# One stream from the output projection through the FFN norm to the first three up units

## The reference

```python
for l in range(DEPTH):                      # DEPTH = 2
    h = pre_mod(x, mix_pre_g[l], sh1, sc1)  # rms_norm(x, g) * (1 + scale) + shift
    y, yc = mixer(h, hc, ...)               # ends in  concat @ w_out  (1024 x 1024)
    x = post_add(x, y, mix_post_g[l], g1)   # x + gate * rms_norm(y, g)
    f = conv_ffn(pre_mod(x, ffn_pre_g[l], sh2, sc2), ffn_w_up[l], ...)
    x = post_add(x, f, ffn_post_g[l], g2)
    # layer 0 does the same for the context tokens xc; layer 1 only reads them
def conv_ffn(h, w_up, conv_w, conv_b, w_down):
    u = h @ w_up                            # 1024 x 5376
    u = three-tap convolution of u along the tokens, plus conv_b
    a, b = split(u, 2)
    return (gelu(a) * b) @ w_down
```

## Time and profile before

| | us |
|---|---|
| median of 3 runs | 1652.82 (1651.49 to 1652.85) |
| the profiled execution, its own time | 1657.06 |
| its span | 1655.3 |
| TensorE busy | 1518.8 |
| VectorE, ScalarE, GpSimd busy | 968.6, 728.8, 596.9 |

### The profile page before, as it was taken

One profiled execution on the slowest core, in us unless ns is written; L12 is line 12 of the kernel. 1 busy time (PEld: TensorE's weight loads), 2 busy tenths in 40 slices (PEclk: granted clock), 3 DMA queues, 4 the chain that ended last, 5 costly groups with the idle time before them and its releaser, 6 DMA issues.

```text
span 1655.3 us, 22238 instructions
## 1 busy us (share of the span) xinstructions
PE 1518.8 (92%) x7560; PEld 1216.7 (74%) x7560; DVE 968.6 (59%) x1465; ACT 728.8 (44%) x1240; POOL 596.9 (36%) x529
## 2 busy tenths in 40 slices
PE   6889798889999999998999698889988899999998
PEld 1777466667888888886888577677776688887886
DVE  2448577557678666833334566688775544444455
ACT  3432466535323333323353445377774544443453
POOL 1342244233222222322333531364442444443454
PEclk9999799999999999999999899899999899999999
DMA  8120750104355344411122112010001233332232
GB/s 329 47 84 13 248 188 25 51 1 132 123 178 153 115 126 140 127 39 39 63 66 63 53 52 80 25 50 1 1 1 51 77 102 89 101 98 67 83 96 101
DMA packets 129135, 143.85 MB, mean 87 GB/s; under 512 B 7160, under 2 KB 95484, under 8 KB 129064
## 3 DMA queue, kind: packets, MB, share of 16 engines
q1 hardware_dynamic: 129064, 142.91, 27.6%
HBM read 140.79 MB, written 2.10 MB: 86 GB/s over the span
## 4 chain that ended last, share of the span: by engine, by line
PE 79%; DVE 8%; ACT 5%; POOL 3%; issue 2%; DMA 2%; SPq 0%; POOLq 0%; DVEq 0%; ACTq 0%
PE ps L462 22%; PE ps L463 22%; PE ps L464 22%; PE ps L1400 3%; PE ps L1386 2%; PE ps L1411 1%; ACT pT_hi L1451 1%; DVE hT_lo L781 1%; DVE hT_hi L779 1%; ACT prob L1440 1%; DMA start_w<-in_ada_w_dram 1%; PE ps L1413 1%; PE ps L666 1%; DVE o_tmp L1516 1%; DMA ada_w<-in_ada_w_dram 1%
## 5 line engine op out<-in xcount | busy, mean ns | idle before, releaser
L454 POOL TENSOR_TENSOR w_lo<-raw,w_hi 128x1024 fp32r<-128x1024 f32 (+1 forms) x184 | 348.0, 1893 | 644.9 <-ACT w_hi L447 644.9
L462 PE MATMUL ps<-hT_hi,w_hi 128*128 128x512 f32 (+1 forms) x1072 | 383.6, 358 | 7.3 <-DVE hT_lo L781 6.4
L463 PE MATMUL ps<-hT_lo,w_hi 128*128 128x512 f32 (+1 forms) x1072 | 381.2, 356 | 0.0
L464 PE MATMUL ps<-hT_hi,w_lo 128*128 128x512 f32 (+1 forms) x1072 | 378.8, 353 | 0.0
L447 ACT ACTIVATE w_hi<-raw 128x1024 fp32r<-128x1024 f32 (+1 forms) x200 | 172.9, 866 | 190.4 <-PE ps L464 166.6
L462 PEld LDWEIGHTS ps<-hT_hi,w_hi 128*128 128x128 f32 x1072 | 202.8, 189 | 46.6 <-DVE hT_lo L781 10.0
L464 PEld LDWEIGHTS ps<-hT_hi,w_lo 128*128 128x128 f32 x1072 | 202.0, 188 | 29.7
L463 PEld LDWEIGHTS ps<-hT_lo,w_hi 128*128 128x128 f32 x1072 | 202.7, 189 | 27.8
L2053 DVE TENSOR_TENSOR g_lo<-act_g,g_hi 128x768 fp32r<-128x768 f32 (+1 forms) x84 | 106.7, 1277 | 164.2 <-ACT g_hi L2003 162.9
L462 PE MATMUL ps<-w_hi,g_hi 128*128 128x512 f32 x420 | 166.0, 395 | 3.5 <-DVE g_lo L2053 3.0
L464 PE MATMUL ps<-w_hi,g_lo 128*128 128x512 f32 x420 | 164.0, 390 | 0.0
(11 more groups left out here) (234 smaller groups left out, 2497.0 us busy)
## 6 DMA issues: line engine op xcount, KB each, us to landing
raw<-in_ffn_w_up_dram SPq DMA_DIRECT2D x84, 512.0 KB, 3.9
ada_w_up<-in_ada_w_dram SPq DMA_DIRECT2D x48, 512.0 KB, 4.1
raw<-in_ffn_w_down_dram SPq DMA_DIRECT2D x84, 256.0 KB, 2.6
ada_w<-in_ada_w_dram SPq DMA_DIRECT2D x32, 512.0 KB, 5.0
start_w<-in_ada_w_dram SPq DMA_DIRECT2D x8, 1024.0 KB, 11.4
raw<-in_c_w_qkv_dram SPq DMA_DIRECT2D x12, 512.0 KB, 3.6
raw<-in_ab_w_in_dram SPq DMA_DIRECT2D x8, 512.0 KB, 4.1
raw<-in_ab_w_out_dram SPq DMA_DIRECT2D x8, 512.0 KB, 3.8
```

Of the source, the lines that this page charges most:

```text
L454: by.tensor_tensor(w_lo[:, slot, 0:width], raw[:, n % RAW, 0:width], w_hi[:, slot, 0:width].bitcast(F32), ALU.subtract).then_inc(lo_split, 1)
L462: nc.tensor.matmul(outp, s_hi, m_hi, start=first, stop=False, skip_group_check=True)
L463: nc.tensor.matmul(outp, s_hi, m_lo, start=False, stop=False, skip_group_check=True)
L464: return nc.tensor.matmul(outp, s_lo, m_hi, start=False, stop=last, skip_group_check=True)
```

## The change

In both layers the two barriers between the output projection and the up units are gone, with the functions that stood between them (`norm_*` for the FFN, `up_prefetch`, `up_first`).

- The last two second halves, (1,4) and (1,5) in layer 0, (1,2) and (1,3) in layer 1, are made together, chunk by chunk, so that the slots of units 4, 5 and 6 come free at chunks 1, 3 and 5; ScalarE splits up units 0 to 2 into them.
- The norm is cut into 12 steps in layer 0 (8 of the four latent tiles, one chunk each; 4 of the two context tiles, two chunks each) and 8 in layer 1 (4 of tiles 0 and 1, 4 of tiles 2 and 3, two chunks each). Each is 4 transposes into one of banks 6, 7, 5. The first three stand within the last batch of the projection.
- TensorE makes the chunks of the first tiles for up units 0, 1 and 2 together, then the rest of unit 0, unit 1, unit 2.
- Every engine's order of the tiles' tails, steps and splits is written out.
- SyncE waits for the gate's last use in place of the barrier.
- In attention VectorE does O ahead of the T before it.

```diff
+def norm_steps(l):
+    if l == 0:
+        return ([((0, 1, 2, 3), 0, k, 1) for k in range(KC)] + [((4, 5), 1, k, 2) for k in range(0, KC, 2)])
+    return [(tiles, 0, k, 2) for tiles in ((0, 1), (2, 3)) for k in range(0, KC, 2)]
...
+def outputs_first(steps):
+    out = list(steps)
+    for n in range(len(out) - 2):
+        if out[n][0] == "T" and out[n + 2][0] == "O":
+            out[n:n + 3] = [out[n + 2], out[n], out[n + 1]]
+    return out
 def attn_vector(dve, l, before):
     groups, steps, first = attn_setup(l)
+    steps = outputs_first(steps)
...
     if l == 1:
-        return [[(1, 0), (1, 1)], [(0, 3)], [(1, 2)], [(1, 3)]]
-    return [[(0, t)] for t in range(OUT_DONE[l], nt)] + [[(1, t)] for t in range(nt)]
+        return [[(1, 0), (1, 1)], [(0, 3)], [(1, 2), (1, 3)]]
+    return [[(0, 4)], [(0, 5)], [(1, 0)], [(1, 1)], [(1, 2)], [(1, 3)], [(1, 4), (1, 5)]]
...
-GATE_BEHIND = (1, 0)
-OUT_BANKS = (0, 1, 2, 3, 4, 5)
+OUT_BANKS = ((1, 3, 0, 2, 4, 5, 1, 3), (0, 2, 4, 1, 3))
+TURN_BANKS = (6, 7, 5)
+TURN_BEHIND = ({5: 0, 6: 1, 7: 2}, {3: 0, 4: 1, 5: 2})
+MID_TILES = (((0, 1, 2, 3), (4, 5)), ((0, 1), (2, 3)))
...
+def mid_turn(pe, l, j):
+    tiles, _, k0, nk = norm_steps(l)[j]
+    tag, w = f"ffn{l}", len(tiles) * P
+    pe.wait_ge(s("norm_xn"), norm_base(tag, "xn") + tiles[-1] + 1)
+    if j >= 3:
+        pe.wait_ge(s("norm_split"), norm_base(tag, "split") + 2 * (j - 2))
+    for i in range(nk):
+        k = k0 + i
+        for n, t in enumerate(tiles):
+            mm = nc.tensor.transpose(bank(TURN_BANKS[j % 3])[:, i * w + n * P:i * w + (n + 1) * P],
+                                     xn[:, t, k * P:(k + 1) * P], ident[:, :])
+    mm.then_inc(s("norm_turned"), 1)
...
+    for n, batch in enumerate(batches):
+        last = n == len(batches) - 1
+        for half, t in batch:
+            if l == 0 and half == 1 and t >= LAT_T:
+                pe.wait_ge(s(f"{tag}_y0"), t + 1)
...
+            if last and k in (1, 3, 5):
+                mm.then_inc(s(f"out{l}_w_used"), 1)
+            if l == 1 and n == 0 and k == 1:
+                gates()
+            if last and k in TURN_BEHIND[l]:
+                if TURN_BEHIND[l][k] == 0:
+                    pe.wait_ge(s(f"{tag}_gate"), 4 if nt == ALL_T else 2)
+                mid_turn(pe, l, TURN_BEHIND[l][k])
+        if l == 0 and n == 1:
+            gates()
...
+def up_first_tensor(pe, l):
+    phase = f"up{l}"
+    steps = norm_steps(l)
+    first = len([g for g in steps if g[0] == MID_TILES[l][0]])
+    def product(u, j, i):
+        tiles, _, k0, _ = steps[j]
+        k, c0, w = k0 + i, tiles[0] * P, len(tiles) * P
+        kk = slice(k * P, (k + 1) * P)
+        return mm3(bank(2 * u, 1024)[:, c0:c0 + w], w_hi[:, u, kk], w_lo[:, u, kk],
+                   hT_hi[:, k, c0:c0 + w], hT_lo[:, k, c0:c0 + w], k == 0 and c0 % BANK == 0, k == KC - 1)
+    for j in range(first):
+        mid_wait_split(pe, l, j)
+        for i in range(steps[j][3]):
+            for u in range(3):
+                if j == 0 and i == 0:
+                    wait_split(pe, phase, u)
+                product(u, j, i)
+        if l == 0 or j + 3 < first:
+            mid_turn(pe, l, j + 3)
+    if l == 1:
+        for j in range(first, first + 3):
+            mid_turn(pe, l, j)
+    for u in range(3):
+        for j in range(first, len(steps)):
+            if u == 0:
+                mid_wait_split(pe, l, j)
+            for i in range(steps[j][3]):
+                mm = product(u, j, i)
+            if u == 0 and j == first:
+                mid_turn(pe, l, first + 3)
+        mm.then_inc(used[phase], 1)
+def mid_shift(act, l, j):
+    tiles, v, k0, nk = norm_steps(l)[j]
+    w = len(tiles) * P
+    act.wait_ge(s("norm_turned"), norm_base(f"ffn{l}", "turned") + j + 1)
+    for i in range(nk):
+        k = k0 + i
+        h = bank(TURN_BANKS[j % 3])[:, i * w:(i + 1) * w]
+        op = nc.scalar.activation(h, h, ACT.Identity, bias=add_col[:, 1, v, k:k + 1],
+                                  scale=mul_col[:, 1, v, k:k + 1])
+    op.then_inc(s("norm_h32"), 1)
...
+def mid_split(dve, l, j):
+    dve.wait_ge(s("norm_h32"), norm_base(tag, "h32") + j + 1)
+    nc.vector.tensor_copy(hT_hi[:, kk, c0:c0 + w], h).then_inc(s("norm_split"), 1)
+    dve.wait_ge(s("norm_split"), norm_base(tag, "split") + 2 * j + 1)
+    nc.vector.tensor_tensor(hT_lo[:, kk, c0:c0 + w], h, hT_hi[:, kk, c0:c0 + w].bitcast(F32),
+                            ALU.subtract).then_inc(s("norm_split"), 1)
...
+    if l == 0:
+        first_half(4)
+        first_half(5)
+        gate_scalar(act, tag, range(4))
+        for t in range(LAT_T):
+            second_half(t)
+            if t:
+                x_square(act, "ffn0", tag, nt, t - 1)
+        up_split(0)
+        x_square(act, "ffn0", tag, nt, 3)
+        up_split(1)
+        mid_shift(act, l, 0)
+        up_split(2)
+        mid_shift(act, l, 1)
+        mid_shift(act, l, 2)
+        second_half(4)
+        second_half(5)
+        mid_shift(act, l, 3)
+        x_square(act, "ffn0", tag, nt, 4)
+        mid_shift(act, l, 4)
+        x_square(act, "ffn0", tag, nt, 5)
+        for j in range(5, len(norm_steps(l))):
+            mid_shift(act, l, j)
+    else:
+        gate_scalar(act, tag, range(2))
+        second_half(0)
+        second_half(1)
+        x_square(act, "ffn1", tag, nt, 0)
+        x_square(act, "ffn1", tag, nt, 1)
+        first_half(3)
+        up_split(0)
+        mid_shift(act, l, 0)
+        mid_shift(act, l, 1)
+        up_split(1)
+        mid_shift(act, l, 2)
+        up_split(2)
+        second_half(2)
+        second_half(3)
+        mid_shift(act, l, 3)
+        x_square(act, "ffn1", tag, nt, 2)
+        x_square(act, "ffn1", tag, nt, 3)
+        for j in range(4, len(norm_steps(l))):
+            mid_shift(act, l, j)
...
 def out_pool(pool, l, nt):
-    post_pool(pool, f"mixpost{l}", nt, f"ffn{l}")
-    close(pool, "pool")
+    tag, then = f"mixpost{l}", f"ffn{l}"
+    early, late = MID_TILES[l]
+    for t in early:
+        post_root(pool, tag, nt, t)
+        if t:
+            x_rms(pool, then, t - 1)
+    x_rms(pool, then, early[-1])
+    split_lo(pool, f"up{l}", 0, 1024)
+    split_lo(pool, f"up{l}", 1, 1024)
+    if l == 0:
+        post_root(pool, tag, nt, late[0])
+    split_lo(pool, f"up{l}", 2, 1024)
+    for t in late[1 - l:]:
+        post_root(pool, tag, nt, t)
+    for t in late:
+        x_rms(pool, then, t)
...
+    if l == 0:
+        first_half_vector(dve, tag, nt, y0)
+        for t in range(LAT_T):
+            gated(t)
+            added(t)
+            if t:
+                x_normed(dve, then, t - 1)
+        x_normed(dve, then, LAT_T - 1)
+        for j in range(3):
+            mid_split(dve, l, j)
+        gated(4)
+        mid_split(dve, l, 3)
+        added(4)
+        gated(5)
+        mid_split(dve, l, 4)
+        added(5)
+        mid_split(dve, l, 5)
+        x_normed(dve, then, 4)
+        mid_split(dve, l, 6)
+        x_normed(dve, then, 5)
+        for j in range(7, len(norm_steps(l))):
+            mid_split(dve, l, j)
+    else:
+        dve.wait_ge(s(f"{tag}_gate"), 2)
+        for t in range(OUT_DONE[1]):
+            first_half_gate(dve, tag, nt, t, y0)
+        for t in (0, 1):
+            gated(t)
+            added(t)
+        x_normed(dve, then, 0)
+        x_normed(dve, then, 1)
+        first_half_gate(dve, tag, nt, 3, y0)
+        for j in range(3):
+            mid_split(dve, l, j)
+        for t in (2, 3):
+            gated(t)
+            added(t)
+        mid_split(dve, l, 3)
+        x_normed(dve, then, 2)
+        x_normed(dve, then, 3)
+        for j in range(4, len(norm_steps(l))):
+            mid_split(dve, l, j)
...
                 if m == 2:
-                    after_phase(sp, 6)
+                    sp.wait_ge(s("mixpost0_post"), post_count(ALL_T, ALL_T - 1, 1))
...
-    turn(0, l == 0, first=1, ada_streams=2)
+    turn(0, l == 0, first=3, ada_streams=2)
...
         out_tensor(pe, l, NT[l])
-        norm_tensor(pe, f"ffn{l}", b + 6, NT[l], 4, up_first(pe, l, NT[l], f"ffn{l}"))
+        up_first_tensor(pe, l)
         up_tensor(pe, l, NT[l])
-        down_tensor(pe, l, b + 8, NT[l])
...
```

More of the change, by code:

```diff
@@ L372, in norm_base @@
         def norm_base(tag, what):
-            nts = [ALL_T, ALL_T, ALL_T, LAT_T][:("mix0", "ffn0", "mix1", "ffn1").index(tag)]
+            tags = ("mix0", "ffn0", "mix1", "ffn1")
+            before = tags[:tags.index(tag)]
             each = {"sq": 1, "xn": 1, "rms": 2}
             if what in each:
-                return sum(each[what] * nt for nt in nts)
-            return sum({"turned": KC, "split": 2 * KC, "h32": KC * (2 if nt == ALL_T else 1)}[what] for nt in nts)
+                return each[what] * ALL_T * len(before)
+            steps = {"mix0": KC, "ffn0": len(norm_steps(0)), "mix1": KC}
+            each = {"turned": 1, "split": 2, "h32": 1}[what]
+            return sum(each * steps[t] * (2 if what == "h32" and t[:3] == "mix" else 1) for t in before)
```

(48 more changed lines are left out.)

206 lines of the change are left out of this document (84 added, 122 removed).

## The result

The changed kernel takes 1645.10 us (median of 5 runs, 1641.98 to 1646.23) against 1652.82 (5 runs, 1651.49 to 1654.48). The ratio is 0.9946, with a 95% interval of 0.9930 to 0.9962: 6 to 12 us faster, 8.9 in the middle. The prediction had 19.4, and its range ended at 1644. Measured again on another chip, beside the kernel before, the changed kernel took 1644.04, ratio 0.9936 (0.9917 to 0.9956).

A forecast was written before the change was run, and what follows sets the result against it. TensorE, with 79% of the chain, was taken as the bound. Gains of 3.0 + 1.3 + 1.5 + 6.0 + 7.6 = 19.4 us, taken from the median of 1652.82, gave 1633.4 us; range 1626 to 1644.

The forecast's parts named there:

- the sum for the first up turn of layer 0: Layer 0, first up turn: VectorE needs 34.9 us less 2.3 of vanishing waits, so its multiply-adds end at 432.15.
- the wait at L1830: End of layer 0's first up turn: TensorE would wait 2.75 us for VectorE's multiply-adds.
- +1.5: Layer 0's stream, output projection to up units: net gain of 1.5 us, bounds -1 and 5.4.
- Where unit 3 starts: Layer 0's up units: unit 3 would start at 404.1 against 409.50, 5.4 us earlier.
- rival C: Norm's first transposes, layer 0: GpSimd takes the shared port first, stream 0.9 to 1.4 us later, 1634.6; chance 0.08.
- Attention, layer 0: Waits for `o_tmp` shrink by 3.0 us (bounds 0 and 4.8), plus 1.3 from less half clock behind the longest gap.
- Attention, layer 1: Nine waits of V for `o_tmp`, 6.5 us in all, shrink by 6.0 us; bounds 0 and 6.5.
- A: Attention: idleness only moves, T waits for `pT_lo` or S for the exponential; 1643.7 us, chance 0.14.
- B: Attention: `pT_lo` is late in every group, up to 0.85 us in some 26 groups; 1665.7 us, chance 0.04.
- Layer 0's stalls: Layer 0's stream: TensorE stalls sum to 7.55 us, the longest 3.85 for unit 2's low half.
- Layer 1's stream: Layer 1, output projection to up units: unit 3 starts 7.6 us earlier, bounds 4 and 9, with stalls of 5.05.
- Rival D: Stream gains nothing because steps of three short queues wait in a ring; only attention pays, 1642.5 us, chance 0.08.

The follow-up runs named there:

- sum_late: Changed kernel, but TensorE sums the multiply-adds of layer 0's first turn behind the first unit of the second turn: 1634.66 us, ratio 0.9873.
- attn_only: Kernel before, with only VectorE's new order in attention (O ahead of the T before it): 1643.93 us, ratio 0.9929.
- l1_order: Changed kernel, but in layer 1 ScalarE makes the high halves of up units 1 and 2 each one shift earlier: 1641.73 us, ratio 0.9921.
- low2_first: Changed kernel, but in layer 0 GpSimd makes unit 2's low half ahead of the root of tile 4: 1639.62 us, ratio 0.9908.
- stream_only: Changed kernel with attention's old order, so only the new order from output projection to up units: 1655.51 us, ratio 0.9997.
- all_four: Changed kernel with five edits: late sum, low halves behind multiply-adds, unit 2's low half earlier, unit 0's behind tile 3's norm, layer 1's ScalarE order: 1628.32 us.

## Why the prediction was wrong

**The step that failed** is the sum for the first up turn of layer 0: "needs 428.4 - 393.5 = 34.9 us, of which some 2.3 are waits that vanish". The 32.6 us that follow were 431.04 - 394.19 = 36.85. VectorE's instructions were taken at the lengths that they had beside the old neighbours. Three multiply-adds met a low half and became 2.10 to 2.15 us longer, 6.4 together; the two gating products and one multiply-add, which had met low halves before, became 0.7, 0.7 and 0.5 us shorter. The start was right: VectorE began this turn 394.19 - 318.39 = 75.8 us behind the last matmul of `ow_gate`, where the walk has 399.55 + 1.1 - 325.21 = 75.4. The prediction had the mechanism in hand and looked for it at one place, the norm's first transposes, where it did happen and did not matter. It also had the wait at L1830 as one of 2.75 us. At 6.49 it brought 2.0 us of half clock, which the sum did not hold. Together with the 0.4 of the start, 4.25 + 2.0 is all of the 6.6 us between +1.5 and -5.06. That it comes out to a tenth is luck, since the stretch varies by some 2 us; that this step is the one is shown by sum_late, which takes away nothing but this wait: by its ratio it is 21.0 us faster than before, where the prediction had 19.4 with a wait of 2.75 in it.

**The number.** Between the two traces the forecast was short by 5.2 us (19.4 against 14.2). The medians differ by 7.7 only. The prediction took its terms from an execution that lay 4.2 us above its median and subtracted them from the median; the execution profiled after the change lay 2.2 below its own. These some 6.5 us are the place of two executions in their spread, and no step of the working holds them.

**Where unit 3 starts.** Forecast 5.4 us earlier, measured 3.6, although the stalls were shorter than forecast. The norm's first transposes came 0.7 late (rival C); no run parts the rest. It did not decide the time of the changed kernel, since TensorE waits for VectorE at the end of the turn.

**Attention, layer 0**: 3.0 + 1.3 forecast, 6.05 measured, the best of the traces (148.5 to 150.8 us for this stretch in the twelve with the new order, 154.6 and 154.9 in the two without). `o_tmp` went from 7.7 to 1.8 us, with 2.5 for ScalarE's `o_low` in its place. The longest gap fell from 2.60 to 1.87 us, as forecast. Behind it the clock did not stay up in every execution: in attn_only, as in the trace after, it was at 0.50 from 309 to 312, for some 3 us against 6.4 in the earlier trace rows. Two readings of the earlier trace rows were wrong. The 0.47 us matmul behind the 1.83 us gap does not show that the clock stayed up: it fell 1.2 us later, and the trace of before has, from 1002.5 on,

```profile
1002.50:1004.00 1.50, 1.50 (x5) 1.11 (x5) 1.50 (x4) 0.00 (x0) 0.28 (x2) 0.50 0.91 307
```

And the gap of 3.53 us before 1529.72 did not lower the clock there: the gates behind it ran at 1.00, in 1.95 us, where four such matmuls took 1.88 and 1.98 at 328.39 and 330.47.

**Attention, layer 1**: 6.0 forecast, 5.4 in this trace. All waits for `o_tmp` before V are gone. **Rivals A and B** fell. A's waits hardly grew: those for the exponential by 0.6 us (15.4 to 16.0 over the span), those of layer 1's T for `pT_lo` were 0.7 before and after. B's shrank: the loads of V's weights waited 17.6 us for `pT_lo` in the two layers before, 3.5 after. And attention alone gave 11.7 us against the 10.3 of the forecast.

**Layer 0's stalls**: 7.55 forecast, 5.53 measured (0.67, 3.54, 0.31, 0.67, 0.34), and 6.9 in l1_order, where the wait for step 5 shows. The first was rival C's, the second had the cause that the prediction's walk through the engines' lists named, as low2_first shows. **Layer 1's stream**: 7.6 forecast, 6.6 measured, and stream_only's 6.5. Its stalls of 1.58 and 1.66 against 1.8 and 1.7 were in the walk; l1_order shows the cause of the first.

**Rival D**, that the stream gives nothing and only attention pays, is what the times show: 1655.51 against 1655.41 for the stream alone. Its reason was another, though. It is not a ring of short queues; layer 1 gains 6.5 us, and layer 0 gives about as much back, at one wait. D had a chance of 0.08, and with it the time would have been 1642.5.

**What stays open.** The last gates, where nothing changed, come behind a gap of 3.53 or 3.54 us in all traces. The four matmuls took 1.95 us in the trace before, in attn_only and in all_four, 3.53 in the trace after, and 2.48 to 3.75 in the other ten. No run tells why one execution loses clock there and another not; it is 1.6 us between the two traces. The 2.1 us between the second turn and layer 1's attention, in code that did not change, I count as the spread of single executions: that stretch lay between 573.7 and 577.7 in the fourteen traces.
